# Gate and up products of a two-block float32 network: each high weight over both input parts in one 512-column product

## The reference

```python
def swiglu(x, w_gate, w_up, w_down):
    h = jax.nn.silu(jnp.einsum('bsd,df->bsf', x, w_gate)) * jnp.einsum('bsd,df->bsf', x, w_up)
    return jnp.einsum('bsf,fd->bsd', h, w_down)

def first_block(x, ...):
    h = x
    for i in range(DEPTH):
        ...        # i = 0: attention; i = 1: short gated convolution; then layer_norm
        h = layer_norm(ALPHA * h + swiglu(h, ffn_w_gate[i], ffn_w_up[i], ffn_w_down[i]),
                       ln2_g[i], ln2_b[i])
    return h
```

## Time and profile before

| | |
|---|---|
| median of 3 runs | 1692.53 us (1692.39 to 1693.0) |
| the profiled execution | 1693.14 us, of which the span of its instructions 1691.8 us |
| TensorE's granted clock, mean | 0.997 of full speed |
| TensorE busy (matmul) | 1663.2 us, 98% of the span |
| VectorE busy | 1085.6 us, 64% |
| ScalarE busy | 853.4 us, 50% |
| GpSimd busy | 594.1 us, 35% |
| share of the chain that ended last | PE 91%, DVE 4%, ACT 2%, DMA 1%, issue 1% |

### The profile page before, as it was taken

How to read it: one execution, slowest core, us unless ns; L and a number is a source line. 1 busy time by engine, 2 the same in 40 slices (tenths; PEclk the granted TensorE clock), 3 DMA queues, 4 the chain that set the end, 5 groups by cost and what they waited for, 6 DMA issues and landing times.

```text
span 1691.8 us, 29567 instructions
## 1 busy us (share of the span) xinstructions
PE 1663.2 (98%) x11502; PEld 1519.3 (90%) x11502; DVE 1085.6 (64%) x1827; ACT 853.4 (50%) x1271; POOL 594.1 (35%) x729
## 2 busy tenths in 40 slices
PE   8989999999999999999999999999999999999998
PEld 6778999899899989887989999999999988888887
DVE  5566555466655536645155798999999555555555
ACT  5566445344544435665454454454455554545454
POOL 0866000030300004555623565555555422222221
PEclk9999999999999999999999999999999999999999
DMA  8334554555555555343345567666555667776775
GB/s 341 141 125 159 203 187 175 203 204 189 192 187 196 182 193 195 119 151 123 125 150 187 190 220 227 203 205 200 176 188 183 215 239 246 237 246 240 243 240 192
DMA packets 97069, 330.62 MB, mean 195 GB/s; under 512 B 10861, under 2 KB 43021, under 8 KB 78369
## 3 DMA queue, kind: packets, MB, share of 16 engines
q1 hardware_dynamic: 94608, 320.71, 55.0%
q0 software_dynamic: 2032, 6.89, 1.3%
q10 hardware_dynamic: 288, 1.11, 0.2%
HBM read 310.32 MB, written 18.35 MB: 194 GB/s over the span
## 4 chain that ended last, share of the span: by engine, by line
PE 91%; DVE 4%; ACT 2%; DMA 1%; issue 1%; POOL 0%; ACTq 0%; DVEq 0%
PE banks L1079 20%; PE banks L533 10%; PE banks L455 8%; PE banks L456 8%; PE banks L457 8%; PE banks L1042 7%; PE banks L1044 7%; PE banks L1043 7%; PE banks L483 3%; PE banks L1029 2%; PE banks L514 2%; PE banks L445 1%; DMA raw<-in_qkv 1%; ACT wH L1115 1%; DVE wL L1695 1%
## 5 line engine op out<-in xcount | busy, mean ns | idle before, releaser
L2457 POOL TENSOR_TENSOR wL<-raw,wH 128x256 fp32r<-128x256 f32 x320 | 243.1, 796 | 554.8 <-ACT wH L1115 545.6
L2233 DVE TENSOR_TENSOR uL<-raw,uH 128x512 fp32r<-128x512 f32 (+1 forms) x255 | 259.0, 1017 | 183.0 <-ACT uH L1597 182.6
L1597 ACT ACTIVATE uH<-raw 128x1024 fp32r<-128x1024 f32 x256 | 270.4, 1056 | 170.2 <-PE banks L1079 167.7
L455 PE MATMUL banks<-xH,wH 128*128 128x256 f32 x1168 | 329.8, 282 | 1.4 <-POOL wL L2457 1.4
L457 PE MATMUL banks<-xH,wL 128*128 128x256 f32 x1168 | 329.0, 282 | 0.0
L456 PE MATMUL banks<-xL,wH 128*128 128x256 f32 x1168 | 328.7, 281 | 0.0
L2494 POOL TENSOR_TENSOR uL<-raw,uH 128x256 fp32r<-128x256 f32 x258 | 245.9, 974 | 229.2 <-ACT uH L1597 229.1
L1695 DVE TENSOR_TENSOR wL<-raw,wH 128x2048 fp32r<-128x2048 f32 (+1 forms) x101 | 228.9, 2272 | 134.0 <-ACT wH L1115 134.0
L1115 ACT ACTIVATE wH<-raw 128x2048 fp32r<-128x2048 f32 (+1 forms) x152 | 267.9, 1772 | 75.5 <-PE banks L533 68.6
L1042 PE MATMUL banks<-xH,uH 128*128 128x256 f32 x1024 | 294.7, 288 | 0.3 <-issue 0.3
L1044 PE MATMUL banks<-xH,uL 128*128 128x256 f32 x1024 | 288.8, 282 | 0.0
(11 more groups left out here) (379 smaller groups left out, 2730.6 us busy)
## 6 DMA issues: line engine op xcount, KB each, us to landing
raw<-in_eu SPq DMA_DIRECT2D x128, 512.0 KB, 3.6
raw<-in_ev SPq DMA_DIRECT2D x128, 512.0 KB, 3.2
raw<-in_gu SPq DMA_DIRECT2D x44, 1024.0 KB, 4.7
raw<-in_dn SPq DMA_DIRECT2D x22, 1024.0 KB, 4.8
gelu_scratch<-st SPq DMA_DIRECT2D x124, 128.0 KB, 3.6
st<-gelu_scratch SPq DMA_DIRECT2D x124, 128.0 KB, 3.1
raw<-in_win SPq DMA_DIRECT2D x14, 1024.0 KB, 4.8
raw<-in_cin SPq DMA_DIRECT2D x12, 1024.0 KB, 4.7
```

The source lines that it names most:

```text
L455: e.matmul(o, wh[:, w0:w0 + P], H[:, k, :], start=k == 0, stop=False)
L1597: e.activation(uH[n % US][:, :], raw[k // 2][:, (k % 2) * UW:(k % 2) * UW + UW], ACT.Copy).then_inc(s_uh, 1)
L2233: e.tensor_tensor(uL[n % US][:, c0:UW], raw[k // 2][:, (k % 2) * UW + c0:(k % 2) * UW + UW], uH[n % US][:, c0:UW].bitcast(F32), ALU.subtra ...
```

## The change

In chunks f = 1 to 21 of both layers the high weight tile meets both input parts in one product. `xH` and `xL` become halves of one tile `xHL`, side by side for each k, so that one product of 512 moving columns (`wide_cols`) gives high weight by high input in columns 0 to 255 of a bank and high weight by low input in columns 256 to 511. The product of the low weights with the high input (256 columns) is added to the first half. Gate takes one bank and up another; chunk f takes banks 4 + 2 (f % 2) and the next. Two chunks' results can stand there instead of four.

The two halves of a bank must then be added. ScalarE copies the second half to SBUF (`fc`), VectorE adds the first half to it (`ft`), once for gate and once for up. Silu reads `ft` instead of PSUM, and `fv` is `sg` times `ft`. TensorE waits for both `ft` of chunk f-2 before chunk f (`s_ft`). Chunk 0 is as before.

Some semaphores are merged to make room for the new ones: `s_sub` into `s_lam`, and `s_c4` into `s_gw`, whose waits count all four small loads now.

```diff
@@ -191,8 +191,9 @@

     raw = [sb(f"raw{i}", [P, CW]) for i in range(2)]
-    xH = sb("xH", [P, KT, S], F32R)
-    xL = sb("xL", [P, KT, S], F32R)
+
+    xHL = sb("xHL", [P, KT, 2, S], F32R)
+    xH, xL = xHL[:, :, 0, :], xHL[:, :, 1, :]
     ident = sb("ident", [P, P])
     mv = sb("mv", [P, 2, 4])
     rs = sb("rs", [P, 2, 4])
@@ -229,6 +230,7 @@
     Og = [sb(f"Og{i}", [P, 4, P], off=o) for i in range(2)]
     mH = sb("mH", [P, KT, S], F32R, off=o)
     mL = sb("mL", [P, KT, S], F32R, off=o)
+    OA = o[0]
     Am = [sb(f"Am{i}", [P, S], off=o) for i in range(2)]
     sm = [sb(f"sm{i}", [P, 8], off=o) for i in range(2)]
     ss = [sb(f"ss{i}", [P, 2, 4], off=o) for i in range(2)]
@@ -241,6 +243,10 @@
     tmp = [sb(f"tmp{i}", [P, D], off=[o[0] + 4096 * i]) for i in range(2)]
     sg = [sb(f"sg{i}", [P, S], off=o) for i in range(2)]
     fv = [sb(f"fv{i}", [P, S], off=o) for i in range(2)]
+
+    fc = [sb(f"fc{i}", [P, 2, S], off=o) for i in range(2)]
+    o = [OA]
+    ft = [sb(f"ft{i}", [P, 2, S], off=o) for i in range(2)]
     o = [OW + 8192]
     yc = sb("yc", [P, KT, S], off=o)
     up = [sb(f"up{i}", [P, S + 2], off=o) for i in range(2)]
...
@@ -464,6 +470,21 @@
                 first_cols(n, bank, H, L, use)
             yield
             cols(n, bank, S, P, H, L, False).then_inc(s_used, 1)
+
+        def wide_cols(n, bank):
+
+            wh, wl = wH[n % NS], wL[n % NS]
+            for q in range(2):
+                o = ps[bank + q]
+                for k in range(KT):
+                    w = slice(k * 256 + q * P, k * 256 + q * P + P)
+                    if q == 0 and k % 4 == 0:
+                        weights(n, k // 4)
+                    if k < KT - 1:
+                        e.matmul(o, wh[:, w], flat2(xHL[:, k, :, :]), start=k == 0, stop=False)
+                    e.matmul(o[:, 0:S], wl[:, w], xHL[:, k, 0, :], start=False, stop=False)
+                r = e.matmul(o, wh[:, w], flat2(xHL[:, k, :, :]), start=False, stop=True)
+            r.then_inc(s_used, 1)
 
         def blocks(n, bank, free, use=None, begin=0):
@@ -747,10 +768,13 @@
         def swiglu(layer, ln, use, more, r):
             n0 = first(f"gu{layer}")
             turn_cols(n0, 4, use, h, lambda j, q: (s_ln, 4 * ln + 2 * j + q + 1), more, 4 * ln + 1)
+
             for f in range(1, FT):
-                if f >= 4:
-                    e.wait_ge(s_fv, FT * layer + f - 3)
-                whole(pair_cols(n0 + f, 4 + f % 4, xH, xL))
+                if f == 2:
+                    e.wait_ge(s_fv, FT * layer + 1)
+                if f >= 3:
+                    e.wait_ge(s_ft, 2 * ((FT - 1) * layer + f - 2))
+                wide_cols(n0 + f, 4 + 2 * (f % 2))
             whole(rows(first(f"dn{layer}"), range(FT // 2), fH, fL, (s_fH, s_fL, [FT * layer + 2 * c + 2 for c in range(FT // 2)]),
                        ((s_mem, more[0] + 1), (s_add, 4 * ln + 2), (s_add, 4 * ln + 3), (s_add, 4 * ln + 4)), 2))
@@ -1331,7 +1355,7 @@
         def swiglu(layer, use, more):
             n0 = first(f"gu{layer}")
             for f in range(FT):
-                b, i, n = 4 + f % 4, f % 2, FT * layer + f
+                b, i, n, m = 4 + 2 * (f % 2), f % 2, FT * layer + f, (FT - 1) * layer + f - 1
                 if f == 0:
                     turn_cols(n0, use, xH, more)
                 else:
@@ -1339,7 +1363,13 @@
                 e.wait_ge(s_used, n0 + f + 1)
                 if f >= 2:
                     e.wait_ge(s_fv, n - 1)
-                e.activation(sg[i][:, :], ps[b][:, 0:S], ACT.Silu).then_inc(s_sg, 1)
+                if f:
+                    for q in range(2):
+                        e.activation(fc[i][:, q, :], ps[b + q][:, S:2 * S], ACT.Copy).then_inc(s_fc, 1)
+                    e.wait_ge(s_ft, 2 * m + 1)
+                    e.activation(sg[i][:, :], ft[i][:, 0, :], ACT.Silu).then_inc(s_sg, 1)
+                else:
+                    e.activation(sg[i][:, :], ps[b][:, 0:S], ACT.Silu).then_inc(s_sg, 1)
                 e.wait_ge(s_fv, n + 1)
                 e.activation(fH[:, f, :], fv[i][:, :], ACT.Copy).then_inc(s_fH, 1)
             exp_ln()
...
@@ -1914,15 +1943,19 @@
         def swiglu(layer, use):
             n0 = first(f"gu{layer}")
             for f in range(FT):
-                b, i, n = 4 + f % 4, f % 2, FT * layer + f
+                b, i, n, m = 4 + 2 * (f % 2), f % 2, FT * layer + f, (FT - 1) * layer + f - 1
                 if f == 0:
                     turn_cols(n0, use, xH, xL)
                 else:
                     split(n0 + f + NS)
+                    for q in range(2):
+                        e.wait_ge(s_fc, 2 * m + q + 1)
+                        e.tensor_tensor(ft[i][:, q, :], ps[b + q][:, 0:S], fc[i][:, q, :], ALU.add).then_inc(s_ft, 1)
+                    e.wait_ge(s_ft, 2 * m + 2)
                 e.wait_ge(s_sg, n + 1)
                 if f >= 2:
                     e.wait_ge(s_fH, n - 1)
-                e.tensor_tensor(fv[i][:, :], sg[i][:, :], ps[b][:, S:2 * S], ALU.mult).then_inc(s_fv, 1)
+                e.tensor_tensor(fv[i][:, :], sg[i][:, :], ft[i][:, 1, :] if f else ps[b][:, S:2 * S], ALU.mult).then_inc(s_fv, 1)
                 e.wait_ge(s_fH, n + 1)
                 e.tensor_tensor(fL[:, f, :], fv[i][:, :], fH[:, f, :].bitcast(F32), ALU.subtract).then_inc(s_fL, 1)
             whole(take_rows(first(f"dn{layer}"), FT // 2, 2))
...
@@ -1792,7 +1822,7 @@
                 e.tensor_tensor(x2, r[0][:, :, 1, :], r[1][:, :, 0, :], ALU.add).then_inc(s_rope, 1)
 
         whole(take_blocks(0))
-        e.wait_ge(s_lam, 16)
+        e.wait_ge(s_lam, 32)
         e.tensor_tensor(lpr[:, :, :], lq[:, 0:2, :], lq[:, 2:4, :], ALU.mult).then_inc(s_dv, 1)
         t = next(own)
         e.wait_ge(s_dv, t)
@@ -1803,7 +1833,6 @@
         e.wait_ge(s_dv, t)
         e.tensor_scalar(lamv[:, 5:6], lamv[:, 4:5], LAM0, None, ALU.subtract).then_inc(s_dv, 1)
         next(own)
-        e.wait_ge(s_sub, 16)
         e.tensor_scalar(sub[:, :], sub[:, :], 1.0 - LAM0, None, ALU.mult).then_inc(s_dv, 1)
         lam_sub = next(own)
         for j in range(2):
@@ -2475,7 +2508,7 @@
         split(cut[3], cut[4])
         sig, v = row_done(R_DN1, "dn1", 3)
         e.wait_ge(sig, v)
-        e.dma_start(ct[:, :, :], a["conv4"]).then_inc(s_c4, 16)
+        e.dma_start(ct[:, :, :], a["conv4"]).then_inc(s_gw, 16)
         e.dma_start(gwt[:, :, :], a["gatew"]).then_inc(s_gw, 16)
         e.dma_start(gbt[:, :], a["gateb"]).then_inc(s_gw, 16)
         e.dma_start(selt[:, :, :], a["sel"]).then_inc(s_gw, 16)
@@ -2529,7 +2562,7 @@
         for n in range(1, NR):
             fetch(n)
         e.dma_start(flat2(lq[:, :, :]), a["lam"].broadcast_to([P, 256])).then_inc(s_lam, 16)
-        e.dma_start(sub[:, :], a["subg"].broadcast_to([P, P])).then_inc(s_sub, 16)
+        e.dma_start(sub[:, :], a["subg"].broadcast_to([P, P])).then_inc(s_lam, 16)
         e.dma_start(nat[:, :, :], a["mem"]).then_inc(s_memd, 16)
         fetch(NR)
         e.dma_start(cst[:, :], a["consts"]).then_inc(s_cst, 16)
```

More of the change, by code:

```diff
@@ L364, in build @@
     s_x = [sem(f"s_x{i}") for i in range(2)]
-    (s_id, s_cst, s_lam, s_sub, s_memd, s_cw, s_c4, s_gw, s_hs, s_gl, s_out) = (
-        sem(n) for n in ("s_id", "s_cst", "s_lam", "s_sub", "s_memd", "s_cw", "s_c4", "s_gw", "s_hs", "s_gl", "s_out"))
+    (s_id, s_cst, s_lam, s_memd, s_cw, s_gw, s_hs, s_gl, s_out) = (
+        sem(n) for n in ("s_id", "s_cst", "s_lam", "s_memd", "s_cw", "s_gw", "s_hs", "s_gl", "s_out"))
     (s_used, s_tp, s_blk, s_row, s_qkp, s_sco, s_apt, s_avo, s_ojn, s_zc, s_gwm, s_gct, s_stl, s_sts, s_sto, s_ejn,
@@ L382, in build @@
          "s_qH", "s_uh", "s_sc", "s_gex", "s_G", "s_ge", "s_gH"))
-    (s_dv, s_eps, s_lov, s_tl, s_lams, s_nrm, s_ln, s_rope, s_sm, s_mx, s_Am, s_on, s_oL, s_add, s_mean, s_fv, s_fL, s_up,
+    (s_dv, s_eps, s_lov, s_tl, s_lams, s_nrm, s_ln, s_rope, s_sm, s_mx, s_Am, s_on, s_oL, s_add, s_mean, s_ft, s_fv, s_fL, s_up,
      s_zv, s_zL, s_gv, s_gcd, s_zm, s_zk, s_za, s_hsm, s_sn, s_eL, s_cvq, s_wt, s_pm, s_mo, s_mn, s_gwl,
@@ L387, in build @@
          "s_dv", "s_eps", "s_lov", "s_tl", "s_lams", "s_nrm", "s_ln", "s_rope", "s_sm", "s_mx", "s_Am", "s_on", "s_oL",
-         "s_add", "s_mean", "s_fv", "s_fL", "s_up", "s_zv", "s_zL", "s_gv", "s_gcd",
+         "s_add", "s_mean", "s_ft", "s_fv", "s_fL", "s_up", "s_zv", "s_zL", "s_gv", "s_gcd",
          "s_zm", "s_zk", "s_za", "s_hsm", "s_sn", "s_eL", "s_cvq", "s_wt", "s_pm", "s_mo", "s_mn", "s_gwl", "s_xm", "s_xp", "s_aL",
@@ L1428, in ml_conv @@
             if c == 0:
-                e.wait_ge(s_c4, 16)
+                e.wait_ge(s_gw, 64)
             for q in range(2):
@@ L1456, in gate_weights @@
         def gate_weights():
-            e.wait_ge(s_gw, 48)
+            e.wait_ge(s_gw, 64)
             e.wait_ge(s_gwl, 1)
```

4 lines of the change are left out of this document (2 added, 2 removed).

## The result

The changed kernel takes 1694.6 us (median of 20 runs), the kernel before 1692.49 us (20 runs beside it): ratio 1.0014, 95% interval 1.0007 to 1.0020. It is slower by about 2 us (1.2 to 3.4), where the prediction had it 1.5 us faster. The profiled execution of the changed kernel took 1694.22 us, against 1693.14.

What follows compares the result with a forecast made beforehand. TensorE was taken to bound the kernel, the change moving the bound to the ring. TensorE saves 3.5 us a layer, 2.7 return as waits: 1.5 us gained in two layers, 1691.0 us; bounds 1688.2 to 1694.6, range reaching 1696.5.

Steps and rivals of the forecast that it cites:

- silu to fv: Step of each chunk from silu's start on ScalarE to the product fv's start on VectorE: 0.46 us.
- the ring: Per-chunk cycle first `ft`, silu, fv, fH, high split, low split, next `ft` on VectorE and ScalarE: 5.81 us, 5.00 before.
- The bound moves from TensorE to the ring of VectorE and ScalarE: Chunks 1 to 21 of each layer: ring of 5.81 us exceeds TensorE's 5.53 and the earlier 5.70.
- the low split to `ft`: Step on VectorE from the start of the low split to the first `ft`: 2.19 us.
- fv to fH: Step from fv's start on VectorE to fH's start on ScalarE: 0.45 us.
- the passage: From silu of chunk 0 starting to the down stage's third chunk starting, the latter forecast at 298.45 us.
- The rival (a): Nothing overlaps on VectorE, plus hundredths for two more fv waits: ring 5.96, 4.5 us lost in all, 1697; chance 0.17.
- TensorE's chunk: 16 wide and 16 narrow products, 226.7 and 118.7 ns each: 5.53 us a chunk, 0.17 less than before.
- The wait in the down stage: TensorE waits once for low weights at the down stage's third chunk, about 1.8 us.
- Copies, fetches, PSUM, merged semaphores at nothing: Copies fit ScalarE's 3 us idle, fetches land early, PSUM counted in TensorE's lead, semaphores nothing within 0.5 us.
- Rival (c): Wide products dearer beside narrow ones, TensorE still binding: 1692.5 at 5.70 a chunk, 41 us more at 6.7; chance 0.04.

Runs made afterwards that it cites:

- Experiment 1: The changed kernel with its wide products taken apart again into 48 products of 256 columns a chunk, copies and sums kept: 1694.31 us, ratio 1.0012.
- Experiment 2: The changed kernel with the high and low splits of later weights moved ahead of `fH` and `fL`: 1688.98 us, ratio 0.9978.
- 6: The changed kernel with a chunk's two sums in the other order, up first, silu waiting for both: 1710.43 us, ratio 1.0115.
- 4: The changed kernel with fv's wait for fH moved ahead of the two sums, its own-sum wait set behind silu's: 1693.05 us, ratio 1.0003.
- 5: The changed kernel with the up half's sum left out, its product copied but not added, fv reading PSUM: 1693.55 us, ratio 1.0000.
- 7: The changed kernel with wide products alone, no copies or sums, the high-by-low product left out of the result: 1689.84 us, ratio 0.9990.

## Why the prediction was wrong

The step that failed is the term "silu to fv" in the sum of the ring: forecast at 0.46 us, measured at 0.51, since a wait now stands between that for silu and fv, and its price was put at nothing. The mechanism, a bound that moves from TensorE to the ring, was right. Point by point:

- **The bound moves from TensorE to the ring of VectorE and ScalarE.** Right. Experiment 1 shows that TensorE's pace no longer counts, 2 that the ring alone takes the gain, 6 that what is added to the ring goes into the time in full, at every step of a layer.
- **The ring is 5.81 us.** Wrong by 0.076. Its parts: 0.05 from silu to fv, 0.02 from the low split to `ft`, 0.01 from fv to fH. The 0.02 stood in the earlier trace rows: behind a low split a small instruction starts after 2.21 us, another low split after 2.19, and I took the 2.19. The 0.05 is the failed step. I saw that fv waits for VectorE's own sum too, compared the ends of the sum (0.75) and of silu (0.87), and took the later. That was the right one, but the wait for the sum, though met, stands behind that for silu in the program, and fv starts 0.09 us after silu's end. Where fv itself waits for silu it is 0.03 (experiments 4 and 5, and the kernel before), and the ring is then 5.827 and 5.823. That silu's wait is not the last any more could be read under "The change": `[waits s_fH,s_sg,s_ft]`.
- **What the longer ring does to the time.** 20 x 0.076 x 2 = 3.0 us, which turns 1.5 us of gain into 1.5 us of loss. The traces show the rest. By the forecast the passage was to be 298.45 - 168.92 = 129.53 us; in the first layer it is 1.76 longer: 1.52 are the 20 steps, 0.08 stand ahead of the first `ft`, 0.05 are once more silu to fv behind the last, and 0.11 lie between the end of the low split and TensorE's product. The second layer has 0.35 more in one step (see the last section). 2 x 1.76 + 0.35 = 3.9 us against the forecast, which leaves 2.3 of loss; the medians say 2.1.
- **What the forecast said of such an error.** The rival (a) named "a few hundredths for two more waits on fv" beside a mechanism that did not happen: the second sum was a step of 0.33 behind the first, and `ft` 2.21 behind the low split, so the overlap on VectorE was there. I put those hundredths into the rival and none into the forecast. The forecast's own bounds for the ring, 5.76 to 5.93, held the measured one, and with it a loss as well as a gain. A ring whose length is multiplied by 40 had no room for that: for any gain against before it had to be below 5.85.
- **TensorE's chunk is 5.53 us.** Wrong: 5.63, since a wide step is 232.8 ns and not 226.7. It did not matter for the time, as experiment 1 shows, only for the waits: the prediction had TensorE wait from the 17th chunk or so, and it waited later and less, 0.3 us each (0.6 in all in the first layer). Where TensorE binds, the wide products save 0.07 us a chunk and not 0.17 (experiments 2 and 7).
- **The wait in the down stage.** Right in place. Its size, 1.6 us before TensorE's product and 2.0 before the load of its operand where 1.8 was forecast, came out by luck: the low weights were there 1.6 us later than forecast (300.07 against 298.45), since the ring was longer, and TensorE had come to them 1.9 us later (298.49 against 296.6), since its chunks were longer.
- **Copies, fetches, PSUM, merged semaphores at nothing.** Nothing in the traces speaks against it. Experiment 2 holds all of them, and its passage is shorter by 2 x 1.43 = 2.9 us, which is what TensorE saves (42 x 0.07). ScalarE's `fc` starts right behind the high split, once it lags, and VectorE never waits for it after chunk 1.
- **Rival (c).** Dearer wide products were the case in part, and had no effect on the time.

Left open: why a wide step depends on k and is 6 ns above that of the down stage, and what made one fv of the second layer late (last section).

## What to carry to other kernels

When work is moved from the engine that binds to others that have idle time, the share of idle time is not enough; write down the cycle that their instruction order forms over one period, and compare its length with the period. If work has to go into it, look for a long step in the cycle that does not depend on the work's result (here the split of later weights) and put it where the engine would wait anyway. A cycle's length must be known to better than the forecast gain divided by the number of periods (here 1.5 us / 40 = 0.04), and waits belong to it, also those that are met: where the wait that ends last is not the last in the program, each one behind it costs, here 0.06 us of the cycle. Read their order in the program and not in the kernel's lines, which here was the reverse.
